# Up parts of the 256-token feed-forwards with standing tokens and 512 moving weight columns

## The reference

```python
def swiglu_ffn(h, w_in, w_out):
    g, u = jnp.split(h @ w_in, 2, axis=-1)
    return (jax.nn.silu(g) * u) @ w_out
```

## Time and profile before

| | us |
|---|---|
| median of 3 runs | 2090.47 (2086.89 to 2092.53) |
| span of the profiled execution | 2082.3 |
| TensorE busy | 2024.0 |
| VectorE busy | 1377.4 |
| ScalarE busy | 940.4 |
| up parts of F1 to F5, first to last product | 134, 134, 132, 133, 132 |

### The profile page before, as it was taken

The page is one execution under the profiler, slowest core; times in us unless marked ns, Lnnn a source line. Parts: engine busy times, 40 slices in busy tenths (PEclk is TensorE's granted clock), DMA queues, the critical chain, the costliest instruction groups (busy, mean ns, idle before and its releaser), DMA issues.

```text
span 2082.3 us, 32485 instructions
## 1 busy us (share of the span) xinstructions
PE 2024.0 (97%) x12969; PEld 1766.2 (85%) x12969; DVE 1377.4 (66%) x1936; ACT 940.4 (45%) x1420; POOL 88.9 (4%) x121
## 2 busy tenths in 40 slices
PE   6999999999999999999999999999999999999999
PEld 4998898998899987569988886688888888878997
DVE  3768798768976776657766756866555335855454
ACT  4344535334643445663355446842222323655342
POOL 1000000000100000310001000010000001100000
PEclk8999999999999999999999999999999999999999
DMA  9897877888877885647954321035344231425553
GB/s 348 277 316 281 297 260 263 302 271 313 273 257 268 303 292 188 226 148 264 303 180 152 113 90 41 12 111 174 130 139 164 81 112 61 142 81 198 180 177 113
DMA packets 240469, 411.32 MB, mean 198 GB/s; under 512 B 10236, under 2 KB 179669, under 8 KB 240341
## 3 DMA queue, kind: packets, MB, share of 16 engines
q1 hardware_dynamic: 239744, 409.31, 57.2%
q10 hardware_dynamic: 597, 0.23, 0.0%
HBM read 408.47 MB, written 1.05 MB: 197 GB/s over the span
## 4 chain that ended last, share of the span: by engine, by line
PE 79%; DVE 12%; ACT 4%; DMA 2%; issue 2%; SPq 0%; POOL 0%; DVEq 0%; ACTq 0%
PE bank L2305 21%; PE bank L2202 14%; PE bank L2204 13%; PE bank L2203 13%; DVE w_lo L1424 3%; PE bank L2395 2%; PE bank L2397 2%; PE bank L2396 2%; DVE gate_b L1480 2%; DMA xs<-in_ada_w 1%; DVE mid L1586 1%; PE bank L2154 1%; PE bank L2566 1%; ACT w_hi L890 1%; DVE astat L1898 1%
## 5 line engine op out<-in xcount | busy, mean ns | idle before, releaser
L1424 DVE TENSOR_TENSOR w_lo<-stage,w_hi 128x2048 fp32r<-128x2048 f32 x255 | 582.1, 2290 | 405.4 <-ACT w_hi L890 405.3
L890 ACT CAST w_hi<-stage 128x2048 fp32r<-128x2048 f32 x255 | 485.7, 1906 | 639.9 <-PE bank L2305 208.9
L2202 PE MATMUL bank<-h_hi,w_hi 128*128 128x256 f32 (+1 forms) x2336 | 699.3, 299 | 0.8 <-DVE w_lo L1424 0.8
L2203 PE MATMUL bank<-h_lo,w_hi 128*128 128x256 f32 (+1 forms) x2336 | 696.3, 298 | 0.0
L2204 PE MATMUL bank<-h_hi,w_lo 128*128 128x256 f32 (+1 forms) x2336 | 696.3, 298 | 0.0
L2202 PEld LDWEIGHTS bank<-h_hi,w_hi 128*128 128x128 f32 x2336 | 447.8, 192 | 14.3 <-DVE w_lo L1424 1.1
L2204 PEld LDWEIGHTS bank<-h_hi,w_lo 128*128 128x128 f32 x2336 | 447.7, 192 | 12.5
L2203 PEld LDWEIGHTS bank<-h_lo,w_hi 128*128 128x128 f32 x2336 | 447.8, 192 | 12.3
L2305 PE MATMUL bank<-w_hi,h_hi 128*128 128x512 f32 x776 | 244.0, 392 | 2.1 <-DVE mid L2066 1.2
L2305 PE MATMUL bank<-w_lo,h_hi 128*128 128x512 f32 x776 | 242.6, 390 | 0.0
L2305 PE MATMUL bank<-w_hi,h_lo 128*128 128x512 f32 x776 | 242.5, 390 | 0.0
(11 more groups left out here) (275 smaller groups left out, 2100.5 us busy)
## 6 DMA issues: line engine op xcount, KB each, us to landing
ada<-in_ada_w SPq DMA_DIRECT2D x114, 1024.0 KB, 5.5
stage<-in_ffn_w_in SPq DMA_DIRECT2D x88, 1024.0 KB, 9.1
stage<-in_ffn_w_out SPq DMA_DIRECT2D x44, 1024.0 KB, 5.1
stage<-in_ffn_w_gu SPq DMA_DIRECT2D x44, 1024.0 KB, 5.2
stage<-in_ffn_w_down SPq DMA_DIRECT2D x22, 1024.0 KB, 4.9
stage<-in_a_w_in SPq DMA_DIRECT2D x12, 1024.0 KB, 7.5
stage<-in_diff_w_in SPq DMA_DIRECT2D x12, 1024.0 KB, 5.4
ada<-in_kv_ada_w SPq DMA_DIRECT2D x8, 1024.0 KB, 7.4
```

Source lines behind the costliest of these rows:

```text
L890: a.copy(w_hi[:, s, :], stage[:, s, :]).then_inc(hi_done, 1)
L1424: v.tensor_tensor(w_lo[:, s, :], stage[:, s, :], w_hi[:, s, :].bitcast(F32), ALU.subtract).then_inc(lo_done, 1)
L2202: m.matmul(dst[:, 0:T], wh, h_hi[:, h0:h0 + T], start=(k == ks[0]), stop=False)
L2203: m.matmul(dst[:, 0:T], wh, h_lo[:, h0:h0 + T], start=False, stop=False)
```

## The change

The up parts of the feed-forwards on 256 tokens (`by_token`) are made the other way round. A unit now holds four of the eight k pieces, for 256 gate and 256 up columns side by side (`pair_unit`, two transfers). The tokens of one tile stand, 512 weight columns move, and a bank receives 256 gate and 256 up columns of 128 tokens. A step is part 0 tile 0, part 0 tile 1, part 1 tile 0, part 1 tile 1, each of 12 matmuls. Silu and its product with up work by token tile (`nat_mid`); four transposes on TensorE (`turn_mid`), placed behind the first twelve matmuls of the next step, and one ScalarE copy (`turned_copy`) bring the result into `mid`. The last step's transposes stand in the down part's first step. Banks: tile `tt` of a step has bank 2 tt or 2 tt + 1, the odd one in steps 1, 4, 7 and 9; transposes go to bank 7 (the last to bank 1). In step 0 tile 0's high products of part 0 come ahead of tile 1's `turn`; ScalarE takes tile 0's lower half instead of the upper one and casts it before tile 1's norm, VectorE makes the upper half during tile 1's norm. One product of the compressed keys moves from bank 7 to bank 5.

```diff
+        def token_bank(s, j, i, tt):
+
+            if j == 0 and i is None and tt and s["xb"] == 0:
+                return bank[6]
+            return bank[2 * tt + (j in (1, 9))]
+
+        def turned_bank(j):
+
+            return bank[1 if j == FC // 2 - 1 else 7]
...
-            return tt == 0 and s["T"] == 256 and (s["n"] == 0 or tight(s) and k >= 4)
+            return tt == 0 and s["T"] == 256 and (s["n"] == 0 or tight(s) and (k < 4) == by_token(s))
...
+            def pair_unit(w, part, c0):
+
+                rows = w[part * D // 2:(part + 1) * D // 2, :].rearrange("(k p) n -> p k n", p=P)
+                return rows[:, :, bass.ds(c0, WCOL)], rows[:, :, bass.ds(c0 + FF, WCOL)]
...
+                if tight(s) and by_token(s):
+                    hi(s, 4, 4, 0)
+                    for k0, n in groups(s, 1):
+                        if k0 == 4:
+                            split(nu + 1)
+                        if k0 < 4:
+                            hi_turned(s, k0, n)
+                        else:
+                            hi(s, k0, n, 1)
+                    return
...
+                def turned_copy(j, i=None):
+
+                    act.wait_ge(mid_turned, s["nat"] + j + 1 + (0 if i is None else i * 3))
+                    o = 2 * j * T if i is None else i * (6 * T) + 2 * j * T
+                    a.copy(mid[:, bass.ds(o, 2 * T)], turned_bank(j)).then_inc(mid_done, 2)
+
+                if by_token(s):
+                    def step(j, i=None):
+                        split(u + 2 * j + 2, i, 6)
+                        if j or i is not None:
+                            turned_copy(j - 1, i)
+                        split(u + 2 * j + 3, i, 6)
+                        for tt in range(2):
+                            if tt == 0:
+                                act.wait_ge(part_done[0], s["sb"][0] + j + 1 + (0 if i is None else i * 3))
+                            else:
+                                act.wait_ge(w_used, u + 2 * j + 2 + (0 if i is None else i * 6))
+                            if j or i is not None:
+                                act.wait_ge(nat_done, 2 * (s["nat"] + j - 1) + tt + 1 + (0 if i is None else i * 6))
+                            a.activation(silu_t[:, tt, 0:T], token_bank(s, j, i, tt)[:, 0:T], ACT.Silu).then_inc(silu_done, 1)
...
+                        for tt in range(2 if by_token(s) else 0):
+                            k = 0 if i is None else i * 6
+                            dve.wait_ge(silu_done, s["sc"] + 2 * j + tt + 1 + k)
...
+                            if j or i is not None:
+                                dve.wait_ge(mid_turned, s["nat"] + j + (0 if i is None else i * 3))
+                            v.tensor_tensor(nat_mid(tt), silu_t[:, tt, 0:T], token_bank(s, j, i, tt)[:, T:2 * T], ALU.mult).then_inc(nat_done, 1)
...
+            def turn_mid(s, j, i=None):
+
+                k = 0 if i is None else i * 3
+                pe.wait_ge(nat_done, 2 * (s["nat"] + j + 1) + 2 * k)
+                if j or i is not None:
+                    pe.wait_ge(mid_done, s["c"] + 2 * j + 2 * k)
+                for c in range(2):
+                    for tt in range(2):
+                        o = (2 * c + tt) * P
+                        ins = m.transpose(turned_bank(j)[:, o:o + P], nat_mid(tt)[:, c * P:(c + 1) * P], ident[:, :])
+                ins.then_inc(mid_turned, 1)
+
+            def token_step(s, j, i, first, also):
+
+                u = s["u"]
+                hi_pass, lo_pass = (False, (w_hi, w_lo)), (True, (w_hi,))
+                for part in range(2):
+                    n = u + 2 * j + part
+                    k = 0 if i is None else i * 6
+                    if not (first and part):
+                        pe.wait_ge(lo_done, n + 1 + k)
+                    for tt in range(2):
+                        dst = token_bank(s, j, i, tt)
+                        last = {0: j - 1, 1: j - 3, 2: j - 2, 9: j - 2, 10: j - 2}[j]
+                        if part == 0 and (i is not None or last >= 0):
+                            pe.wait_ge(nat_done, 2 * (s["nat"] + last) + tt + 1 + k)
+                        args = (s, dst, n % RING, part, tt)
+                        if first and part == 0 and tt == 0:
+                            token_product(*args, (hi_pass,), True, True, False)
+                            if tight(s):
+                                turn(s, 1)
+                            ins = token_product(*args, (lo_pass,), True, False, False)
...
+                        if part == 0 and tt == 0 and (j or i is not None):
+                            turn_mid(s, j - 1, i)
```

More of the change, by code:

```diff
@@ L117, in trace @@
         silu_done = sem("silu_done")
+        nat_done = sem("nat_done")
+        mid_turned = sem("mid_turned")
         mid_done = sem("mid_done")
@@ L229, in norm_col, with by_token, unit_landed @@
             return col_at["norm_g"] + ((layer * 3 + sub) * 2 + which) * KC
-        plan = [("prologue",)]
-        N = dict(unit=0, vec=2, chunk=0, bstep=0, silu=0, step=[0, 0, 0])
+        def by_token(s):
+            return s["kind"] == "ffn" and s["T"] == 256
+        loads = []
+        def unit_landed(n):
+            return 16 * sum(loads[n % RING:n + 1:RING])
+        N = dict(unit=0, vec=2, chunk=0, bstep=0, silu=0, nat=0, step=[0, 0, 0])
         def add(kind, w_in, w_out, T, nvec, v0, g_pre, g_post, weight, steps, parts, bsteps, Td=None):
@@ L248, in add @@
                 N["silu"] += 2 * steps
-            for q in range(parts if kind in ("ffn", "conv") else 0):
+            loads.extend([2 if by_token(s) else 1] * (steps * parts) + [1] * bsteps)
+            if by_token(s):
+                N["nat"] += steps
+            for q in range(1 if by_token(s) else parts if kind in ("ffn", "conv") else 0):
                 N["step"][q] += steps
@@ L1678, in boundary @@
                         x_norm(s, tt)
-                if n_prev:
+                if n_prev and by_token(s):
+                    for f in one[8:16]:
+                        f()
+                    lo_half(s, 0)
+                    split(nu + 1)
+                    lo_half(s, 4)
+                elif n_prev:
                     for f in one[8:] if s["T"] == 256 else pair:
@@ L2233, in pair_product, with token_product @@
                 return ins
+            def token_product(s, dst, slot, part, tt, passes, first, start, stop):
+                tag, T = f"s{s['n']}", s["T"]
+                for n, (lo_, w_) in enumerate(passes):
+                    for kk in range(KC // 2):
+                        k = 4 * part + kk
+                        if first and lo_ and tt and dve_lo(s):
+                            pe.wait_ge(dve_s, t.at(lo_by_dve(s, k, 1)))
+                        elif first and lo_:
+                            pe.wait_ge(pool_s, t.at((tag, "lo", group_of(s, k, tt), tt)))
+                        elif first:
+                            pe.wait_ge(act_s, t.at((tag, "hi", group_of(s, k, tt), tt)))
+                        r = s["hb"] + k * T + tt * P
+                        for m_, wx in enumerate(w_):
+                            ins = m.matmul(dst[:, :], (h_lo if lo_ else h_hi)[:, r:r + P], wx[:, slot, kk * 2 * WCOL:(kk + 1) * 2 * WCOL],
+                                           start=start and n == 0 and kk == 0 and m_ == 0,
+                                           stop=stop and n == len(passes) - 1 and kk == KC // 2 - 1 and m_ == len(w_) - 1)
+                return ins
@@ new lines, in token_step @@
+            def token_step(s, j, i, first, also):
+                u = s["u"]
+                hi_pass, lo_pass = (False, (w_hi, w_lo)), (True, (w_hi,))
+                for part in range(2):
+                    n = u + 2 * j + part
[13 more added lines that the diff above has]
+                            ins = token_product(*args, (lo_pass,), True, False, False)
+                        elif first and part and tt == 0:
+                            pe.wait_ge(hi_done, n + 1)
+                            token_product(*args, ((False, (w_hi,)), lo_pass), True, False, False)
+                            pe.wait_ge(lo_done, n + 1)
+                            ins = token_product(*args, ((False, (w_lo,)),), True, False, True)
+                        else:
+                            ins = token_product(*args, (hi_pass, lo_pass), first, part == 0, part == 1)
+                        if tt:
+                            ins.then_inc(w_used, 1)
+                        elif part:
+                            ins.then_inc(part_done[0], 1)
+                        if part == 0 and tt == 0 and (j or i is not None):
+                            turn_mid(s, j - 1, i)
+                        for f in (also or {}).get((part, tt), ()):
+                            f()
@@ L2762, in block3 @@
                                 first_step_pairs(s)
+                            elif by_token(s):
+                                token_step(s, j, i, first, also)
```

90 lines of the change are left out of this document (60 added, 30 removed).

## The result

The changed kernel takes 2096.96 us (median of 11 runs, 2093.7 to 2099.79), the kernel before 2089.85 us beside it (11 runs, 2085.18 to 2096.6). The ratio is 1.0036, 95% interval 1.0025 to 1.0048: 7.1 us slower, a little over what a measurement tells from no change. The forecast was 2093.0, with 2079 to 2103 as its range.

What follows compares the result with a forecast made beforehand. TensorE, busy 2024.0 of 2082.3 us, was taken as the bound. Terms -35.2 + 24.8 + 8.0 + 11.0 - 6.0 = +2.6 us gave a span of 2084.9 and a forecast of 2093 us; range 2079 to 2103, its own 2086 to 2097.

Steps and rivals of the forecast that it cites:

- Base: Whole kernel: the runs' median, 2090.47, lies 8.2 us above the profiled span, taken as launch and end.
- A: Up-part products: 48 at 0.2267 us replace 96 at 0.12; saves 0.64 us a step, 35.2 over 55 steps.
- B: Turning results: four more TensorE transposes per step, 0.11 us each, 0.45 together, +24.8 us over 55 steps.
- D: Loop turn, mainly step 6: TensorE waits for tile 0's bank until VectorE's product of silu and up; +11.0 us.
- C: Start of the down part: its first product waits for the second gate copy, 1.6 us five times, +8.0 us.
- rival 1: Loop waits melt as VectorE's chain follows TensorE: without D 2082, without C too 2074 us; chance 0.28.
- rival 2: Steps 3, 6 and 9 wait if split transfers land 1.5 us later: up to 12 us more, 2105; chance 0.19.
- E: First step: products of tile 0 fill TensorE's idle time ahead of tile 1's turn; -6.0 us, bounds 0 and -9.
- Rival 3: First step: ScalarE's reordering eats the gain of E, 2099 us; chance 0.08.
- The down parts: Five down parts, each taking the last step's four transposes: 0.45 us each, counted within B.
- Slower by over 0.3%: Whole kernel: a measurement above 2096.7 us, from rival 2 and most of Rival 3; chance 0.25.
- The named test: Last 256-token feed-forward: forecast is wrong if it alone doesn't gain about 2.8 us (A, B and E, less 1.6).

Runs made afterwards that it cites:

- gates_first: Changed kernel, but in step 10 ScalarE copies the gate behind silu of tile 0 instead of tile 1; ratio 1.0012 to the kernel before.
- short_loads: Changed kernel, but in looped steps each modulation vector's weight transfer brings 256 of its 1024 columns; ratio 1.0006 to the kernel before.
- third_bank: Changed kernel, but tile 0 of the last step of each loop pass goes to bank 6; ratio 0.9992 to the kernel before.
- two_transfers: Kernel before, with each w_in unit of the 256-token feed-forwards loaded in two transfers of 512 KB instead of one; ratio 1.0002 to the kernel before.
- gpsimd_later: Changed kernel, but GpSimd's low half of tile 0 waits until VectorE has normed tile 1's second half; ratio 1.0027 to the kernel before.
- only_the_last: Kernel with gate copies earlier, a third bank and GpSimd later, but only the last 256-token feed-forward goes by token; ratio 0.9982 to the kernel before.
- turn_before_products: Changed kernel, but in F2, F4 and F5 TensorE turns tile 1 before tile 0's first eight products; ratio 1.0064 to the kernel before.
- transposes_twice: Changed kernel with each of the four transposes of results issued twice; 2118.22 us, ratio 1.0135 to the kernel before.

## Why the prediction came out as it did

**Base, wrong.** It took the 8.2 us between the median and the span as launch and end. That is 1.7 to 2.1; the rest was a quick execution (granted clock 0.991, where other runs had down to 0.986). It did no harm, because differences were added to the median.

**A, right.** 0.227 at 512 columns. The rule weighed against it (the Trainium skill, TensorE: Matmul & The Clock Gate, section Back-to-back issue gap, where it stands for isolated products) would have put the sum 28.6 us higher, some 2122; neither the distances nor the time allow that.

**B, too cheap by some 3 us.** A plain step takes 11.36 for the 11.33 that A and B gave: a gain of 0.16, not 0.19. The steps that also turn a vector or the gate gain only 0.02 to 0.14, and those right behind a wait lose 0.05 to 0.09. The prediction left these other eight transposes at their old price and a wait at its bare length; but behind such a break in the stream the first wide product has its successor at 0.31 to 0.34 instead of 0.227. From step 1 on, the waits of D aside, the fifty steps gained 6.5 us where 9.5 were forecast, and 0.9 of it is the wait in F2's step 8 that the kernel before had in this profile.

**C, right.** 8.25 for 8.0, and gates_first shows the mechanism in the rows: it was the order on ScalarE alone, and nothing stood behind it. By the time the undoing gave 5.0, with 8.2 not excluded.

**D, mechanism right, size off both ways.** 7.8 us of waits for 11.0: F1 0.5 for 2.2, F2 3.7 for 4.4, F3 0.8 for 2.1, F4 2.9 for 2.3. Part of VectorE's chain did move forward with TensorE, as rival 1 said, but only part, as short_loads shows. What was missing is the price behind a wait: 1.6 us of half clock in F4's step 6 (14.01 us long; the same step is 12.44 long in F2, where the clock held). With it D is 9.4. The margin at step 3, which the forecast put at 0.5 us, held in F1, F3 and F4 and was passed by 0.4 in F2; in four other profiles F1's step 3 waited as well, for 0.8 to 1.3 us (third_bank, above). The sign that the prediction named for rival 2, idle time at step 3 too, is therefore there, though it costs 1 or 2 us and not 12; nothing speaks for its cause, split transfers (two_transfers). The idle time at step 6 of F1 and F3, 0.5 and 0.8 us, is under the 2 to 3.5 that the prediction named as D's sign.

**E, right in kind, too large.** The gain is there, but smaller. These are the times from the last product ahead to the start of step 1, and what is left without A's 0.64 (us):

| | before | after | E | forecast |
|---|---|---|---|---|
| F1 (from 0) | 52.16 | 50.60 | 0.9 | 0.6 |
| F2 | 19.90 | 18.38 | 0.9 | 1.2 |
| F3 | 18.99 | 18.39 | 0.0 | 0 |
| F4 | 19.88 | 18.05 | 1.2 | 1.9 |
| F5 | 22.16 | 19.83 | 1.7 | 2.3 |

Together 4.6 for 6.0, and F1's is within what its start varies. Rival 3, the whole gain eaten, is out. The step that failed put the turn of tile 1 0.65 us later than before, counting only ScalarE's cast. In F4 the first half of that turn came 0.4 us later (5.96 us behind the last product ahead, 5.58 before), the second half another microsecond. ScalarE's cast also starts GpSimd's second low half just as VectorE norms the second half of tile 1, which costs 1.0 us. The prediction did not look at GpSimd at all. It explains 1.0 us each in F4 and F5 (gpsimd_later) and nothing in F2, whose 0.3 stays open.

**The down parts, 1.2 us too cheap.** Those of F1, F2, F3 and F5 grew by 0.57 to 0.62 where 0.45 were counted. In gates_first, where no gap stands ahead of them, F1's and F3's grew by just 0.45 (60.98 for 60.53): the other 0.12 goes with C's gap and the slower first products behind it. F4's grew by 1.1. There the wait ahead of the last turned vectors varies from profile to profile: the part took 66.15 in gates_first, but also 65.17 in only_the_last, where F4 is computed as before, so the 0.5 over the others' growth isn't shown to be the change's.

The sum was +2.6 and 6.8 was measured in these places: B 3.0, E 1.4, the down parts 1.2 and C 0.25 more, D 1.6 less, together 4.2. So the sign and the order of size came from the mechanisms, but that the miss stayed at 4 us is in part luck: the waits of D came out 3.2 us shorter than forecast, which paid for the half clock (1.6) and for 1.6 of the 5.9 that the other terms missed. The time of 2096.96 lies at the upper edge of the forecast's own range (2086 to 2097), inside the full one. "Slower by over 0.3%" had 0.25; the measured 0.36% is just there, and its interval includes 0.3. The named test, F5 alone gaining 2.8 us, came out at 2.12 us up to its down part and 0.59 lost in it, 1.5 us. By the prediction's own sign that is a miss of 1.3 us: 0.6 of it is E's, 0.4 B's, most of the rest the down part's.

## What to carry to other kernels

Halving the number of products, from 256 to 512 moving columns, paid 13 ns for each product left out, and turning the results took most of it back. What then decides are the new ends of waits: after such a turn-over, list what now becomes ready only with a step's last product, and put the short jobs others wait for (here two copies) ahead of it. Where a loop's length is no multiple of the number of banks, look at the turn of the loop: one more bank was worth as much as the whole change in products.

## What the runs showed of the hardware

A wait of TensorE can cost more than its length: products behind it may run at half clock. Nine waits at step 6 were over 2 us from product to product (2.29 to 3.43) in the five kernels that have them; behind six of them products ran at half clock for a while, and the step was 1.5 to 2.8 us longer. Behind waits at steps 3, 6 and 9 of up to 1.78 us it was never seen. The two levels are 2.4 and 1.2 GHz: 0.227 and 0.43 us from product to product. Two nearly equal waits, F2's in the changed kernel (3.00, clock 1.00 behind it) and in gates_first (3.10, clock 0.57 behind it):

```profile
415.00:420.00 5.00, 5.00 (x24) 4.12 (x25) 0.26 (x1) 1.47 (x1) 0.00 (x0) 1.00 1.10 348
```
```profile
415.00:420.00 5.00, 5.00 (x17) 3.99 (x16) 1.46 (x1) 2.36 (x2) 0.00 (x0) 0.57 1.10 348
```

In the second window 17 products started, in the first 24. The rule for it can't be read from these nine. The clock held behind 3.00 and 2.98 (turn_before_products) and fell behind 2.29 (transposes_twice), so the length of the wait alone doesn't decide.

VectorE's 128x512 instruction took 1.50 to 1.53 us beside GpSimd's low half and 0.48 without it, at the same place in F2, F4 and F5. GpSimd had started 0.04 us before it (1898.17 and 1898.21) and ended at 1899.43, VectorE 0.28 us behind that. GpSimd's own took 1.26 us, no longer than alone (1.29). So it looks as if the two did not share, and the one stood still until the other was done. The Trainium skill says this of the two engines' common port pair (SBUF — State Buffer, section SBUF: two separate sides): if VectorE's instruction is of a kind that uses the pair, whoever starts first has it for the whole instruction. The times agree with it; in which mode VectorE's instruction ran, no row shows.
